# A transformer block on one core: turning probabilities and queries with DVE and DMA instead of TensorE

## The chip, the cores and the metric

The kernel runs on one core of a Trainium2 chip. The metric is the device time of one execution in microseconds (us). TensorE (PE) multiplies, VectorE (DVE), ScalarE (ACT) and GpSimd (POOL) work element by element, SyncE (SP) issues DMAs.

## The reference

One block on a sequence of 256 tokens of width 2048, in float32, followed by a sliding-window attention. Cut to what is computed:

```python
h = x
y = rms(h) ; z = y @ w_in                      # 2048 x 4096
oa, ob, oc, od = four mixers on parts of z     # gated unit, two convolutions, pooling
h = h + concat(oa, ob, oc, od) @ w_out         # 2048 x 2048
y = rms(h) ; h = h + (silu(y @ w_gate) * (y @ w_up)) @ w_down      # 2048 x 5632 and back
y = rms(h) ; h = h + sigmoid(y @ w_ple_gate) * (p @ w_ple_proj)    # 2048 x 2048
h = rms(h)
# attention: 32 heads of 64 in 4 groups, one key/value head per group, window 128
q, k, v, gate = split(rms(h) @ swa_w_in)       # 2048 x 4608
s = rms(q) @ rms(k).T * scale + bias[bucket(distance)]     # blocks of 128 queries x 256 keys
p = exp(s - max(s, sink)) / (sum + exp(sink - max))
out = h + ((p @ v) * silu(gate)) @ swa_w_out   # 2048 x 2048
```

## The kernel before, in words

**Weights.** All weight matrices pass through TensorE in 500 chunks of 256 rows x 512 columns (512 KB). SP loads chunk `s` into `w_raw` (8 slots, `RAW`), ACT rounds it to fp32r in `w_hi` (`split` at L542, 4 slots, `SPL`; the high part), DVE subtracts that from the raw one into `w_lo` (`split` at L867; the low part), and PE makes 12 matmuls of 128x512 from both (`chunk`, L1373 to L1375: low weights, high weights, and high weights with the low part of the activations). ACT waits for PE to be done with chunk `s-4` before it writes the high part of chunk `s`, so ACT and DVE can be up to four chunks ahead of PE. A unit is 8 chunks: 512 output columns.

**Order.** Each engine has its own list, written out by hand: for every chunk `(v, c)` (unit `v`, chunk `c` of it) first the chunk, then what else stands at that place. ACT, DVE and SP wait only by semaphores, in list order. Nothing is reordered.

**Attention.** The attention's input projection is units `v` = 0 to 8, chunks 396 to 467. Unit 0 gives keys and values, units 1 to 4 the queries of head groups `g` = 0 to 3, units 5 to 8 their gates. Head group `g` is worked on from unit `v = g + 3` on, in three rounds (`ROUNDS`): round 0 is the first 128 queries (8 heads, 128 keys), rounds 1 and 2 the last 128 queries (4 heads each, 256 keys). A round is a chain over three engines:

- `score` (PE, L1593) multiplies queries and keys into the banks `sp`;
- `softmax_max` (DVE, L1225 to L1233) adds the bias, finds the largest value and gives the maximum to ACT;
- `exp` (ACT, L772) takes the exponentials in `tile2` or `tile6`, by turns;
- `turn` (PE, `blocks`, L1403) transposes the 128x1024 probabilities in 8 matmuls against the identity, `copy` (ACT, L596) brings them into `tile7`;
- `weigh` (PE, L1614) multiplies them with the values into a bank `tp`, `keep_output` (ACT, L782) copies that out.

The queries are transposed on PE as well (`to_features`, L1393, 8 matmuls) and copied by ACT with their gain (`copy`, gqk). `denominators` (DVE, L1241) sums up. POOL squares the queries (L528), makes their inverse norms (L500, L502) and loads the bias of the next head group.

Elsewhere a 256x512 piece is transposed without PE: `turn` on DVE (L889, 32x32 blocks), then `move` on SP: one DMA to `parked` in DRAM and four back (the blocks put in place).

**Gate of the embedding (`PLE_UNIT`).** Four units before the attention, one after the other. Its first three input pieces are turned by DVE and DMA, the fourth by PE (`H_PLE`, 8 matmuls).

## Time and profile before

| | us |
|---|---|
| median of 3 runs | 1438.45 (1437.99 to 1438.53) |
| the profiled execution's own time | 1438.18 |
| its span, first to last instruction | 1436.4 |
| PE busy | 1428.5 (99%) |
| DVE busy | 881.7 (61%) |
| ACT busy | 702.2 (49%) |
| POOL busy | 52.5 (4%) |

The granted clock of TensorE was 1.00 over the whole span. PE's busy time is modelled from pipelined matmuls: of two matmuls the second starts 0.23 us after the first and each is drawn 0.39 us long, so what a piece of work costs PE is read from start to start, not from the busy column. The attention stage, where most of the change lies, is 1163 to 1313 us of the span; the unit of head group `g` = 2, used below as the example, starts near 1236.

### The profile page before, as it was taken

How to read it: one execution, taken by the hardware profiler on the slowest of the kernel's cores; microseconds unless marked ns; L12 is line 12 of the kernel's file. 1: busy time of each engine (PE TensorE's matmuls, PEld its weight loads, DVE VectorE, ACT ScalarE, POOL GpSimd, SP SyncE). 2: the span in 40 equal slices, each digit the busy share in tenths (PEclk: the TensorE clock that was granted, in tenths of full speed). 3: DMA queues.
4: the chain of work that ended last, by engine and by line, in shares of the span. 5: the costliest groups of instructions: out<-in, count | busy, mean ns of one | idle time of the engine just before them, and what ended most of it. 6: DMA issues, size and time to landing. Idle time of an engine off the chain costs nothing.

```text
span 1436.4 us, 17816 instructions
## 1 busy us (share of the span) xinstructions
PE 1428.5 (99%) x6495; PEld 1171.8 (82%) x6495; DVE 881.7 (61%) x1138; ACT 702.2 (49%) x942; POOL 52.5 (4%) x52
## 2 busy tenths in 40 slices
PE   9999999999999999999999999999999999999999
PEld 7888888888888888888888888888888877777887
DVE  5599976665555554545555545557677666676653
ACT  7444555454444433444443344445556566675442
POOL 2000010000000000000000000000000222110000
PEclk9999999999999999999999999999999999999999
DMA  9766557676766666677665667767677655546762
GB/s 333 224 190 174 179 178 251 216 257 199 231 210 226 223 191 192 193 225 222 220 220 196 193 194 220 222 223 241 230 237 236 208 189 162 169 142 201 264 221 89
DMA packets 160212, 301.28 MB, mean 210 GB/s; under 512 B 10673, under 2 KB 26285, under 8 KB 160024
## 3 DMA queue, kind: packets, MB, share of 16 engines
q1 hardware_dynamic: 158328, 293.76, 64.1%
q0 software_dynamic: 1792, 6.71, 1.5%
q8 instruction: 38, 0.62, 0.2%
q14 instruction: 22, 0.18, 0.0%
q10 hardware_dynamic: 32, 0.01, 0.0%
HBM read 284.65 MB, written 15.78 MB: 209 GB/s over the span
## 4 chain that ended last, share of the span: by engine, by line
PE 96%; DVE 2%; ACT 1%; issue 0%; DMA 0%; ACTq 0%
PE acc L1373 31%; PE acc L1375 30%; PE acc L1374 30%; PE acc L1435 1%; PE tp L1393 1%; PE tp L1614 1%; PE sp L1593 1%; PE tp L1403 1%; ACT tile L772 1%; DVE w_lo L867 1%; DVE tile L1225 0%; ACT w_hi L542 0%; DVE smx L1229 0%; DMA resid<-in_x 0%; PE tp L1425 0%
## 5 line engine op out<-in xcount | busy, mean ns | idle before, releaser
L867 DVE TENSOR_TENSOR w_lo<-w_raw,w_hi 128x1024 fp32r<-128x1024 f32 x500 | 612.4, 1227 | 509.4 <-ACT w_hi L542 508.5
L542 ACT ACTIVATE w_hi<-w_raw 128x1024 fp32r<-128x1024 f32 x500 | 528.7, 1060 | 628.4 <-PE acc L1375 626.5
L1373 PE MATMUL acc<-w_lo,yh 128*128 128x512 f32 x1184 | 461.4, 390 | 0.0
L1375 PE MATMUL acc<-w_hi,yl 128*128 128x512 f32 x1184 | 460.7, 389 | 0.0
L1374 PE MATMUL acc<-w_hi,yh 128*128 128x512 f32 x1184 | 460.6, 389 | 0.0
L1373 PE MATMUL acc<-w_lo,hh 128*128 128x512 f32 x784 | 309.2, 394 | 0.0
L1374 PE MATMUL acc<-w_hi,hh 128*128 128x512 f32 x784 | 305.4, 390 | 0.0
L1375 PE MATMUL acc<-w_hi,hl 128*128 128x512 f32 x784 | 305.4, 390 | 0.0
L1373 PEld LDWEIGHTS acc<-w_lo,yh 128*128 128x128 f32 x1184 | 222.2, 188 | 46.8 <-issue 0.6
L1375 PEld LDWEIGHTS acc<-w_hi,yl 128*128 128x128 f32 x1184 | 222.2, 188 | 46.1
L1374 PEld LDWEIGHTS acc<-w_hi,yh 128*128 128x128 f32 x1184 | 222.3, 188 | 46.0
L1373 PEld LDWEIGHTS acc<-w_lo,hh 128*128 128x128 f32 x784 | 147.1, 188 | 38.9 <-issue 8.6
L1375 PEld LDWEIGHTS acc<-w_hi,hl 128*128 128x128 f32 x784 | 147.2, 188 | 31.1
L1374 PEld LDWEIGHTS acc<-w_hi,hh 128*128 128x128 f32 x784 | 147.2, 188 | 29.3
L945 DVE SCALAR_TENSOR_TENSOR tile<-tile,cw 128x255 f32<-128x255 f32 (+29 forms) x120 | 48.3, 471 | 0.0
L500 POOL TENSOR_SCALAR eps_ms<-ms 128x2 f32<-128x2 f32 (+2 forms) x9 | 5.4, 601 | 958.3 <-DVE ms L929 916.2
L772 ACT ACTIVATE tile<-tile,negm 128x128 f32<-128x128 f32 (+1 forms) x64 | 28.3, 446 | 16.3 <-DVE ssink L1233 16.3
L549 ACT ACTIVATE tile<-acc,rs 128x512 f32<-128x512 f32 x42 | 26.3, 677 | 4.4 <-PE acc L1375 4.4
L923 DVE TENSOR_TENSOR resid<-acc,resid 128x512 f32<-128x512 f32 x38 | 24.4, 683 | 0.0
L502 POOL TENSOR_TENSOR rs<-eps_ms,minus_half 128x2 f32<-128x2 f32 (+2 forms) x12 | 24.0, 1999 | 1.0
L1225 DVE SCALAR_TENSOR_TENSOR tile<-sp,rs,big 128x128 f32<-128x128 f32 (+1 forms) x64 | 21.9, 409 | 2.6 <-PE sp L1593 2.6
L596 ACT ACTIVATE tile<-tp 128x512 f32<-128x512 f32 x30 | 16.1, 587 | 14.4 <-PE tp L1403 8.3
(151 smaller groups left out, 518.9 us busy)
## 6 DMA issues: line engine op xcount, KB each, us to landing
w_raw<-in_w_gate SPq DMA_DIRECT2D x88, 512.0 KB, 4.4
w_raw<-in_w_up SPq DMA_DIRECT2D x88, 512.0 KB, 4.5
w_raw<-in_w_down SPq DMA_DIRECT2D x88, 512.0 KB, 4.3
w_raw<-in_swa_w_in SPq DMA_DIRECT2D x72, 512.0 KB, 4.0
w_raw<-in_w_in SPq DMA_DIRECT2D x64, 512.0 KB, 4.5
w_raw<-in_w_out SPq DMA_DIRECT2D x32, 512.0 KB, 4.5
w_raw<-in_w_ple_gate SPq DMA_DIRECT2D x32, 512.0 KB, 5.2
w_raw<-in_swa_w_out SPq DMA_DIRECT2D x32, 512.0 KB, 5.1
```

Source lines behind the costliest of these rows:

```text
L502: pool.tensor_tensor(rs[:, k, 0:n], eps_ms[:, k, 0:n], minus_half[:, 0:n], ALU.pow).then_inc(got, 1)
L542: act.activation(w_hi[:, s % SPL], w_raw[:, s % RAW], ACT.Copy).then_inc(hi_ready, 1)
L549: last = act.activation(dst[:, t], acc[u % 2][t][:], func, scale=s_)
L596: act.activation(dst[:, 512 * i:512 * (i + 1)], tp[(h + i) % 2][:], ACT.Copy, scale=scale).then_inc(tp_left["a"], 1)
L772: act.activation(sv[:, i], sv[:, i], ACT.Exp, bias=negm[:, n, i:i + 1], accum_out=ssum[:, n, i:i + 1])
L867: dve.tensor_tensor(w_lo[:, s % SPL], w_raw[:, s % RAW], w_hi[:, s % SPL].bitcast(F32), ALU.subtract).then_inc(lo_ready, 1)
L923: last = dve.tensor_tensor(cols, acc[u % 2][t][:], cols, ALU.add)
L945: dve.scalar_tensor_tensor(dst, src, w_, dst, ALU.mult, ALU.add).then_inc(conv, 1)
L1225: last = dve.scalar_tensor_tensor(sv[:, i], src, rs[:, R_Q + g, 8 * t + h:8 * t + h + 1], bias[:, h, 0:w][:, ::-1], ALU.mult, ALU.add)
L1373: pe.matmul(dst, xh[:, f, tk], w_lo[:, s % SPL, k], start=(f == 0), stop=False)
L1374: pe.matmul(dst, xh[:, f, tk], w_hi[:, s % SPL, k], start=False, stop=False)
L1375: last = pe.matmul(dst, xl[:, f, tk], w_hi[:, s % SPL, k], start=False, stop=(f == CK * n - 1))
```

## The change

- **Probabilities.** After `exp`, DVE transposes 32x32 blocks (`turn_probs`, one instruction of 128x1024), SP writes them to DRAM (`put_probs`) and reads them back with the blocks in place (`fetch_probs`, four DMAs). The 8 PE transposes and the two ACT copies of each of the 12 rounds are gone. `weigh` moves back in PE's list: round 0 from `(v,3)` to `(v,7)`, round 1 from `(v,6)` to `(v+1,1)`, round 2 from `(v+1,1)` to `(v+1,3)`.
- **Queries.** The same for the four query tiles (`turn_queries` on DVE, `put_queries` and `fetch_queries` on SP), then ACT scales them into place (`queries_in_place`, at `(v,1)`, where the copy stood at `(v,0)`).
- **Buffers.** Two of the three probability buffers are weight slots: from chunk 396 on, weights turn through 6 slots of `w_raw`, not 8.
- **POOL.** In each of the units 3 to 6 the low parts of chunks 4 and 6 are made by POOL (`weights_low`).
- **Gate units woven.** The four units of the embedding's gate are taken in the order `DOWN` (6 chunks of unit 0, 6 of unit 1, then the rest of both), and the fourth input piece is turned by DVE and DMA too: 8 PE transposes less.
- SP's moves are cut into a put and a later fetch.

```diff
+ATT = START[SWA_UNIT]
+ATT_SLOTS = [(ATT + i) % RAW for i in range(RAW - 2)]
+SPARE_SLOTS = [(ATT - 2) % RAW, (ATT - 1) % RAW]
+POOL_LOW = [ATT + 8 * v + c for v in range(3, 7) for c in (4, 6)]
...
+                    if c == 1 and 3 <= j <= 6:
+                        put_queries(j - 3)
...
+                    if c == 3 and 3 <= j <= 6:
+                        fetch_queries(j - 3)
+                    if c == 3 and 4 <= j <= 7:
+                        put_probs(3 * (j - 4))
...
+                    if c == 5 and 4 <= j <= 7:
+                        fetch_probs(3 * (j - 4))
+                        put_probs(3 * (j - 4) + 1)
...
+            def weights_low(i):
+
+                for s in POOL_LOW[2 * i:2 * i + 2]:
+                    pool.wait_ge(hi_ready, s + 1)
+                    pool.tensor_tensor(w_lo[:, s % SPL], w_raw[:, slot(s)], w_hi[:, s % SPL].bitcast(F32),
+                                       ALU.subtract).then_inc(low_by_pool, 1)
...
+            def queries_in_place(g):
+
+                act.wait_ge(q_in, 64 * (g + 1))
+                if g:
+                    act.wait_ge(scores, 3 * g)
+                src = queries.rearrange("p (q k t n) -> p k t q n", q=4, k=4, t=T)
+                for t in range(T):
+                    last = act.activation(quarters(feat(4))[:, :, t], src[:, :, t], ACT.Copy, scale=gqk[:, 0:1])
+                last.then_inc(q_ready, 1)
...
-                    if c == 0 and 3 <= v <= 6:
-                        copy(H_Q[v - 3], tile[4], gqk[:, 0:1])
...
-                        copy(H_PT[v - 4, 2], tile[7])
+                    if c == 0 and 5 <= v <= 8:
+                        keep_output(v - 5, 2)
+                    if c == 1 and 3 <= v <= 6:
+                        queries_in_place(v - 3)
...
+            def turn_probs(g, r):
+
+                n = 3 * g + r
+                dve.wait_ge(expd, n + 1)
+                if n >= 3:
+                    wait_half(dve, H_PV[g - 1, r])
+                dve.transpose(probs[n % 3].rearrange("p (r b n) -> p b r n", r=4, n=32),
+                              tile[(2, 6)[n % 2]][:].rearrange("p (b r n) -> p b r n", r=4, n=32)).then_inc(p_blocks, 1)
...
                     if c == 1 and 4 <= v <= 7:
+                        turn_probs(v - 4, 2)
                         denominators(v - 4, 2)
                     if c == 1 and 3 <= v <= 6:
                         softmax_max(v - 3, 0)
+                    if c == 3 and 2 <= v <= 5:
+                        turn_queries(v - 2)
                     if c == 3 and 3 <= v <= 6:
                         softmax_max(v - 3, 1)
...
                     if c == 5 and 3 <= v <= 6:
+                        turn_probs(v - 3, 0)
                         softmax_max(v - 3, 2)
...
                     if c == 7 and 3 <= v <= 6:
+                        turn_probs(v - 3, 1)
                         denominators(v - 3, 1)
...
                 if r == 0:
-                    wait_half_left(pe, H_Q[g] + 1)
+                    pe.wait_ge(q_ready, g + 1)
...
                     if c == 1 and 4 <= v <= 7:
+                        weigh(v - 4, 1)
+                    if c == 2 and 3 <= v <= 6:
+                        score(v - 3, 2)
+                    if c == 3 and 4 <= v <= 7:
                         weigh(v - 4, 2)
```

DVE's list from the low part of chunk `(v,7)` to the next group's first bias addition, before (L867 is a low part, `rden` the denominators, `ms` the query norms, `sp` the scores):

```order
L867 TENSOR_TENSOR w_lo<-w_raw,w_hi 128x1024
L1208 TENSOR_REDUCE ms<-tile 128x16
L1241 TENSOR_TENSOR rden<-ssum,ssink 128x4
L1242 RECIPROCAL rden<-rden 128x4
L867 TENSOR_TENSOR w_lo<-w_raw,w_hi 128x1024 x2
L1241 TENSOR_TENSOR rden<-ssum,ssink 128x4
L1242 RECIPROCAL rden<-rden 128x4
L1225 SCALAR_TENSOR_TENSOR tile<-sp,rs,big 128x128 x8
```

The same stretch of DVE's list now (L967 is the low part, L1330 `turn_probs`):

```order
L967 TENSOR_TENSOR w_lo<-w_raw,w_hi 128x1024
L1330 STREAM_TRANSPOSE w_raw<-tile 128x8x4x32
L1365 TENSOR_TENSOR rden<-ssum,ssink 128x4
L1366 RECIPROCAL rden<-rden 128x4
L967 TENSOR_TENSOR w_lo<-w_raw,w_hi 128x1024 x2
L1330 STREAM_TRANSPOSE w_raw<-tile 128x8x4x32
L1365 TENSOR_TENSOR rden<-ssum,ssink 128x4
L1366 RECIPROCAL rden<-rden 128x4
L1349 SCALAR_TENSOR_TENSOR tile<-sp,rs,big 128x128 x8
```

Two transposes stand in the stretch that had none; the query norms have moved one chunk forward.

ACT's list from the exponentials of round 2 to those of the next group's round 0, before (L542 is a high part, L596 with `gqk` the queries, other L596 the probabilities, L782 `keep_output`):

```order
L774 ACTIVATE ssink<-ssink 128x4
L782 ACTIVATE wide<-tp 128x4x128
L542 ACTIVATE w_hi<-w_raw 128x1024
L596 ACTIVATE tile<-tp 128x512 x2
L542 ACTIVATE w_hi<-w_raw 128x1024
L596 ACTIVATE tile<-tp,gqk 128x512 x2
L542 ACTIVATE w_hi<-w_raw 128x1024
L782 ACTIVATE wide<-tp 128x2x128
L542 ACTIVATE w_hi<-w_raw 128x1024
L596 ACTIVATE tile<-tp 128x512 x2
L772 ACTIVATE tile,ssum<-tile,negm 128x128 x8
```

The same stretch of ACT's list now (L635 is the high part, L886 `queries_in_place`):

```order
L868 ACTIVATE ssink<-ssink 128x4
L635 ACTIVATE w_hi<-w_raw 128x1024 x2
L877 ACTIVATE wide<-tp 128x2x128
L635 ACTIVATE w_hi<-w_raw 128x1024
L886 ACTIVATE tile<-wide,gqk 128x4x128 x2
L635 ACTIVATE w_hi<-w_raw 128x1024
L866 ACTIVATE tile,ssum<-tile,negm 128x128 x8
```

The copies of the probabilities are gone; the queries are made ready after three high parts instead of two.

## Rows read from the trace of the kernel before

**Rows 1.** Stretch 1197:1230: busy us and count of each engine, clock, DMA share, GB/s.

```profile
1197.00:1230.00 33.00, 33.00 (x182) 24.69 (x181) 21.79 (x44) 21.77 (x56) 7.22 (x5) 1.00 0.54 159
```

**Rows 2.** Waits of PE in the attention stage: us in total, times, longest.

```profile
PE tp L1403 <- ACT wide L782: 2.3, 2, 1.5
```

**Rows 3.** Timeline of PE: start us, us, what, xcount.

```profile
1226.44 0.40 PE L1375 MATMUL acc<-w_hi,hl 128*128 128x512 f32 x1
1226.67 1.04 PE L1393 MATMUL tp<-ident,tile 128*128 128x128 f32 x8
...
1227.78 0.39 PE L1374 MATMUL acc<-w_hi,hh 128*128 128x512 f32 x1
...
1230.41 1.16 PE L1593 MATMUL sp<-tile 64*128 64x128 f32 x16
...
1263.24 0.49 PE L1593 MATMUL sp<-tile 64*128 64x128 f32 x4
```

**Rows 4.** Timeline of ACT, head group 2, from the exponentials of round 0.

```profile
1236.99 0.40 ACT L772 ACTIVATE tile<-tile,negm 128x128 f32<-128x128 f32 x1
...
1240.17 1.05 ACT L542 ACTIVATE w_hi<-w_raw 128x1024 fp32r<-128x1024 f32 x1
1241.12 1.25 ACT L549 ACTIVATE tile<-acc,rr 128x512 f32<-128x512 f32 x2
...
1245.80 0.51 ACT L772 ACTIVATE tile<-tile,negm 128x256 f32<-128x256 f32 x1 [0.24 <-DVE ssink L1233]
...
1247.88 1.04 ACT L542 ACTIVATE w_hi<-w_raw 128x1024 fp32r<-128x1024 f32 x1
...
1253.50 0.51 ACT L772 ACTIVATE tile<-tile,negm 128x256 f32<-128x256 f32 x1 [2.67 <-DVE ssink L1233]
...
1255.59 0.57 ACT L782 ACTIVATE wide<-tp 128x512 f32<-128x512 f32 x1
```

**Rows 5.** Timeline of DVE, head group 2.

```profile
1231.67 2.16 DVE L1225 SCALAR_TENSOR_TENSOR tile<-sp,rs,big 128x128 f32<-128x128 f32 x8 [0.60 <-PE sp L1593]
...
1241.25 1.22 DVE L867 TENSOR_TENSOR w_lo<-w_raw,w_hi 128x1024 fp32r<-128x1024 f32 x1 [4.55 <-ACT w_hi L542]
1242.39 1.65 DVE L1225 SCALAR_TENSOR_TENSOR tile<-sp,rs,big 128x256 f32<-128x256 f32 x4
...
1250.10 1.65 DVE L1225 SCALAR_TENSOR_TENSOR tile<-sp,rs,big 128x256 f32<-128x256 f32 x4
...
1259.49 0.15 DVE L1241 TENSOR_TENSOR rden<-ssum,ssink 128x4 f32<-128x4 f32 x1
...
1259.88 1.22 DVE L867 TENSOR_TENSOR w_lo<-w_raw,w_hi 128x1024 fp32r<-128x1024 f32 x1
```

**Rows 6.** Timeline of DVE, block transposes and a low part beside POOL.

```profile
1147.56 1.30 DVE L889 STREAM_TRANSPOSE wide<-tile 128x512 f32<-128x512 f32 x2
1148.78 1.18 DVE L867 TENSOR_TENSOR w_lo<-w_raw,w_hi 128x1024 fp32r<-128x1024 f32 x1
1150.30 2.50 DVE L867 TENSOR_TENSOR w_lo<-w_raw,w_hi 128x1024 fp32r<-128x1024 f32 x1 [0.34 <-ACT w_hi L542]
```

**Rows 7.** Timeline of POOL: the squares of head groups 0 and 2.

```profile
1148.79 2.93 POOL L528 TENSOR_TENSOR tile<-tile 128x1024 f32<-128x1024 f32 x1 [3.87 <-ACT tile L549]
...
1242.44 1.90 POOL L528 TENSOR_TENSOR tile<-tile 128x1024 f32<-128x1024 f32 x1 [11.37 <-ACT tile L549]
```

**Rows 8.** DMA issues, whole span: count, KB each, median us to landing.

```profile
parked<-tile SPq DMA_DIRECT2D x25, 512.0 KB, 5.1
tile<-parked SPq DMA_DIRECT2D x100, 128.0 KB, 2.7
```

**Rows 9.** Head group 0's first exponential (ACT).

```profile
1171.38 0.40 ACT L772 ACTIVATE tile<-tile,negm 128x128 f32<-128x128 f32 x1 [2.61 <-DVE ssink L1233]
```

**Rows 10.** Table loads of ACT beside `exp`, 1163:1310: count, busy us, mean ns.

```profile
L772 ACT ACT_TABLE_LOAD x2 | 2.6, 1283 | 0.0
```

**Rows 11.** Timeline of PE: first matmul of chunk (7,4).

```profile
1313.16 0.39 PE L1373 MATMUL acc<-w_lo,hh 128*128 128x512 f32 x1
```

More of the change, by code:

```diff
@@ L170, in build @@
     parked = nc.dram_tensor("parked", (P, 1024), F32, kind="Internal").ap()
+    parked_q = nc.dram_tensor("parked_q", (P, 1024), F32, kind="Internal").ap()
+    parked_p = [nc.dram_tensor(f"parked_p{i}", (P, 1024), F32, kind="Internal").ap() for i in range(3)]
     with ExitStack() as ctx:
@@ L277, in build @@
         turned = sem("turned")
+        low_by_pool = sem("low_by_pool")
+        p_blocks = sem("p_blocks")
+        p_out = [sem(f"p_out{i}") for i in range(3)]
+        p_in = [sem(f"p_in{i}") for i in range(3)]
+        q_blocks = sem("q_blocks")
+        q_out = sem("q_out")
+        q_in = sem("q_in")
+        q_ready = sem("q_ready")
         blocks_out = sem("blocks_out")
@@ L292, in wait_unit, with wait_low @@
             eng.wait_ge(used, LAST_CHUNK[u] + 8 * lap.oct)
+        def wait_low(eng, s, lap=ONCE):
+            if s in POOL_LOW:
+                eng.wait_ge(low_by_pool, POOL_LOW.index(s) + 1)
+            else:
+                eng.wait_ge(lo_ready, s + 1 - sum(1 for i in POOL_LOW if i < s) + 8 * lap.oct)
         def taker(h):
```

317 lines of the change are left out of this document (169 added, 148 removed).

## The prediction

> **What bounds the kernel now.** I read the page first: PE is 99% busy, all else far from full, and the granted clock is 1.00. Next the stretches of the attention stage: in one period of 33 us DVE and ACT are each 21.8 us busy and the DMA share is 0.54, so nothing but PE is near its limit [rows 1]. Third, PE's waits: in the whole stage 2.3 us, two waits of PE's transposes for ACT's `keep_output` [rows 2]. So PE's own work is the end of the kernel: what leaves PE's list is a gain, as long as the others deliver in time. Last I followed one period through ACT and DVE, since the change gives DVE work and takes away PE's: that decides here. The period of a head group is 1263.24 - 1230.41 = 32.83 us [rows 3].
>
> **What leaves PE.** From the last matmul before a group of 8 transposes (1226.44) to the second one behind it (1227.78) are 1.34 us; without the group these would be two steps of 0.23 [rows 3]. A group costs 1.34 - 0.46 = 0.88 us. The change removes 12 groups of probabilities, 4 of queries, 1 of the embedding's gate: 17 x 0.88 = 15.0 us, and the two waits, 2.3. Where round 0's `score` stood right before a `weigh` (1230.41 and the group at its end), both now stand alone, an estimated 0.2 us each for switching in and out, three times: -0.6. If nothing else came late, the profiled execution would go from 1438.18 to 1438.2 - 15.0 - 2.3 + 0.6 = 1421.5 us. PE's work in a period would be 32.83 - 4 x 0.88 + 0.2 = 29.5 us.
>
> **What then comes late: the ring of `softmax_max` and `exp`.** ACT and DVE hold the softmax and the parts of the weights in one list each, so the three rounds of a group and the first of the next are one ring, which can't turn faster than its own sum. I count from the first exponential of round 0 (1236.99 in the example).
>
> Leg 1, to the first exponential of round 1. Exponentials 1236.99 to 1240.17: 3.18. High part, then DVE's low part, beside it ACT's `take` (1241.12 + 1.25): until 1242.39, 2.22. New: `turn_queries`, two 128x512 block transposes, which start the next instruction 1148.78 - 1147.56 = 1.22 later [rows 6]. They stand before round 1's bias additions and wait for the `take`, which ends at the same moment. Then softmax, 1242.39 to the exponential at 1245.80: 3.41. Sum 10.03, before 8.81 [rows 4, 5].
>
> Leg 2, to round 2. Exponentials 2.08 (1245.80 to 1247.88), high and low part 2.22 (1247.88 to 1250.10), new `turn_probs` of round 0: one 128x1024 transpose, taken as the pair, 1.2. Softmax 1250.10 to 1253.50: 3.40. Sum 8.90, before 7.70 [rows 4, 5].
>
> Leg 3, to the next group's round 0. Exponentials 2.09 (1253.50 to 1255.59); high and low part of chunk 7, 2.22; `turn_probs` 1.2; denominators 0.39 (1259.49 to 1259.88); low parts of chunks 0 and 1, 2 x 1.14 (as 1241.25 to 1242.39) = 2.28; `turn_probs` of round 2, 1.2; denominators 0.39; softmax of round 0, 3.41 + 2.16 - 1.65 = 3.92. Sum 13.69. Before, it took 32.83 - 8.81 - 7.70 = 16.32: there DVE waited for ACT, whose list held three pairs of copies and waits for PE's transposes. So the removed copies pay here, and DVE becomes the one behind which ACT stands [rows 3 to 5].
>
> The ring: 10.03 + 8.90 + 13.69 = 32.6 us. The old period is 32.83. The gain of 3.3 us per period on PE is nearly all given back: PE waits 32.6 - 29.5 = 3.1 us in each, and I can say where. `queries_in_place` comes after three high parts (0.95 each, 1240.17 to 1241.12) and takes about 1.25 as the `take` does, so round 0's `score` of the next group is released at 10.03 + 8.90 + 2.09 + 2.85 + 1.25 = 25.1 us of the ring. The first group has no `weigh` beside it. Its own first `score` stands 1.26 (1230.41 to 1231.67) + 3.92 = 5.2 us before its first exponential, at 1170.5 (below), and PE needs from there 3 scores of about 1.25 and 8 chunks of 2.72, 25.5 us: it is back at 1190.8, and the release is at 1170.5 + 25.1 = 1195.6: a gap of 4.8 us [rows 3, 5].
>
> **What is left of the gain.** The low parts were ready well before PE wanted them; that lead is used up, once. In the clock of the old trace: group 0's first exponential comes 0.88 earlier (its query transposes go), at 1171.38 - 0.88 = 1170.5 [rows 9]. Three turns of 32.62 bring group 3's to 1268.4. Its leg 1 has no query transposes but two table loads of 1.28 [rows 10] (the gate's `take` is a silu) and lasts about 9.7; leg 2 8.9; exponentials, high and low part 2.09 + 2.22: the low part of chunk (6,7) is ready at 1291.3. PE waits for it, needs 2.72 for the chunk (12 x 0.227, the step of rows 3) and then wants round 0's turned probabilities at 1294.0. Their fetch stands behind the load that waits for that same low part: issued at 1291.3, 2.7 to land [rows 8], and the fourth is issued after the first, I take 4: 1295.3. Then three `weigh` of about 1.2 and four chunks: chunk (7,4) starts at 1295.3 + 3.6 + 10.9 = 1309.8, where it was 1313.16 [rows 11]. That is 3.4 us, with 0.88 of the embedding's gate 4.2. Behind it the list is PE's alone, as before. 1438.18 - 4.2 = 1434.0 us; the old median is 0.3 above the profiled execution, which I leave aside.
>
> **The other parts.** POOL's eight low parts, 8 x 1.22 us off DVE, are not on the ring's sum (the stretch around chunks 4 and 6 has none on DVE now), but without them it would be 2.3 us longer per turn. POOL took 1.90 us for 128x1024 with one tensor read twice and 2.93 beside a low part of DVE [rows 7]; PE wants chunk 4 over 5 us after its high part, so POOL itself hides at either price. The block transposes to and fro: a put lands in 5.1, a fetch in 2.7 [rows 8]; queries are put near 8 us of the ring, fetched near 14 and needed near 24, cover 5 us and more. The six slots instead of eight: a load is issued when the low part six chunks earlier is done and has over 10 us until its high part; a put of as many bytes lands in 5.1 [rows 8]. DMA traffic rises from 0.54 of the time by four moves of 1 MB on 5.2 MB per period, to about 0.54 x 9.4 / 5.2 = 0.97 if the small packets cost as the mean does, and less if as weights: that is near full, and the one place where cover could vanish. `weigh` now reads its moving operand in runs of 32 instead of 128 elements; no row shows that. From nothing to a doubling of 1 us per `weigh`; I take nothing, since PE has 3 us to spare per period, and keep +2 us for the last three. The woven gate units: 0.88 gained, the turned piece has five chunks of 2.72 for 5.1 + 2.7.
>
> **A rule against it.** While POOL squared the queries of group 0, DVE's low part took 2.50 instead of 1.22, and POOL 2.93 instead of 1.90; group 2's square lay beside a bias addition (one operand in PSUM) and both kept their time [rows 5 to 7]. By this rule, the trace agrees. The Trainium skill, "GPSIMD Engine Reference", Specifications, says that GpSimd shares its SBUF interfaces with VectorE and that it contends with DVE instructions in a two-port mode or with two SBUF inputs. By my walk POOL's low parts run at 7 to 9 and 14 to 16 us of the ring, where DVE has bias additions, reductions and a transpose, so the sum keeps 1.22.
>
> **Rivals.**
>
> PE stays the bound: the ring turns faster than I count (transposes cheap, ACT ahead), and most of 16.7 us arrives: 1421.5 to 1431. For it: all views show PE as the bound. Against: every item but the transposes is a start-to-start of the trace, and to reach 29.5 the three block transposes and the queries' 1.22 would have to cost 0.4 us each. Chance 0.15.
>
> Not much changes: the DMA load near 0.97 delays a fetch by 2 us per group, or the gaps of 3 to 5 us on PE, longer than any wait of before (1.5, rows 2), let its clock fall from 2.4 to 1.2 GHz. A chunk at the lower level takes 2.72 us more. In the first three groups that hides (PE is 3 us early again), behind the last gap it doesn't: 1434.0 + 2.7 = 1436.7. The Trainium skill, "TensorE: Matmul & The Clock Gate", section "Why this matters for your kernels", warns of such gaps between bursts; no row here shows a fall. Within 0.2% (about what a measurement of this kernel tells from no change): 1435.6 to 1441.3. Chance 0.15.
>
> Slower, by the shared port: POOL's low parts and square slide onto DVE's low parts of chunks 3, 5 and 7. Each meeting adds 2.50 - 1.22 = 1.28 to the ring. Two per turn in 3.3 turns are 8.4: 1442.4; three 1446.6. It decides from 2.2 us per turn on. For it: DVE is to be 21.8 + 4 x 1.2 - 2 x 1.22 = 24 us busy of 32.6. Against: the places above. Chance 0.15.
>
> **Numbers.** The ring as counted 0.55, with 1431 to 1437.5 (each of the four transposes off by 0.2 moves 2.6 us), of it 0.13 within 0.2%. Faster 0.42 + 0.15 = 0.57, same 0.13 + 0.15 = 0.28, slower 0.15. The range that leaves out the far ends: 1426 to 1441.
>
> **What would show it.** Right: PE waits of 3 to 5 us before round 0's `score` for ACT's `queries_in_place`, in units 3 to 5; the same group's first exponentials 32.6 apart; DVE without pause from the low part of chunk 7 to round 0's softmax; margin of the low parts before PE near zero at chunk (6,7). Wrong: scores less than 31 us or more than 34 apart; PE waits named for DMAs; low parts of 2.5 us on DVE; a clock below 1.00.

## The result: slower by 0.45%, and the profile after

The changed kernel takes 1444.86 us (median of 6 runs, 1442.79 to 1446.56), the kernel before 1438.19 in the runs beside it (1437.99 to 1438.53). The ratio is 1.0045, with a 95% interval of 1.0034 to 1.0056: 6.7 us slower. The forecast was 1434.0 us (1426 to 1441) and faster. The profiled execution took 1445.09 us, its span 1443.4, which is 7.0 more than before.

The stretches of the attention stage after, the columns as in [rows 1] (busy us and count of PE, PEld, DVE, ACT, POOL; granted clock, DMA share, GB/s):

```profile
1163.00:1197.00 34.00, 28.84 (x135) 22.40 (x133) 21.88 (x41) 20.53 (x51) 10.43 (x6) 0.95 0.63 193
1197.00:1230.00 33.00, 30.62 (x141) 22.21 (x142) 24.22 (x47) 18.64 (x52) 11.09 (x7) 0.90 0.92 290
1230.00:1263.00 33.00, 30.25 (x146) 21.45 (x145) 24.23 (x48) 18.73 (x51) 10.87 (x7) 0.95 0.90 279
1263.00:1296.00 33.00, 31.26 (x158) 22.50 (x157) 25.42 (x46) 21.51 (x53) 4.88 (x2) 1.00 0.82 258
1296.00:1320.00 24.00, 18.22 (x85) 12.83 (x83) 16.73 (x21) 11.59 (x14) 0.00 (x0) 1.00 1.03 302
```

The second row answers to [rows 1]: PE executes 141 matmuls where it executed 182 (recorded ones), DVE is busy 24.22 us as forecast (24), and the DMA share is 0.92 instead of 0.54. PE's waits in the stage, the answer to [rows 2]:

```profile
PE sp L1714 <- ACT tile L886: 8.1, 3, 4.1
PE tp L1730 <- DMA tile<-parked_p: 7.0, 3, 3.0
PE tp L1730 <- DMA w_raw<-parked_p: 2.8, 2, 1.9
```

2.3 us have become 17.9. The first line (`score` for `queries_in_place`) was forecast; the 9.8 us of the other two, `weigh` waiting for its probabilities to land, were not, and are one of the signs that the prediction had named for being wrong. The last row of the table above has a granted clock of 1.00: from 1263 us on nothing of the loss is the clock's.

Where the time is lost can be read off five starts of ACT: round 0 of the four head groups and round 2 of the last (start, us, instruction).

```profile
1173.92 0.40 ACT L866 ACTIVATE tile<-tile,negm 128x128 f32<-128x128 f32 x1 [3.83 <-DVE ssink L1357]
...
1206.62 0.40 ACT L866 ACTIVATE tile<-tile,negm 128x128 f32<-128x128 f32 x1 [6.44 <-DVE ssink L1357]
...
1239.34 0.40 ACT L866 ACTIVATE tile<-tile,negm 128x128 f32<-128x128 f32 x1 [6.18 <-DVE ssink L1357]
...
1272.06 0.40 ACT L866 ACTIVATE tile<-tile,negm 128x128 f32<-128x128 f32 x1 [5.11 <-DVE ssink L1357]
...
1291.68 0.51 ACT L866 ACTIVATE tile<-tile,negm 128x256 f32<-128x256 f32 x1 [4.72 <-DVE ssink L1357]
```

They cut the stage into four pieces that can be compared in every kernel: the start of the first exponential, three turns of the ring, two more legs in group 3, and the tail from there to chunk (7,4), after which PE's list is full in these two (123.2 us to the end of the span before, 123.3 after). The prediction counts 1170.5 and 1309.8 in the clock of the old trace and takes the 0.88 us of the gate units off at its end; in the table they are taken off at once, so that its column can be set beside a trace.

| us | before | forecast | after |
|---|---|---|---|
| first exponential | 1171.38 | 1169.6 | 1173.92 |
| three turns | 98.4 | 97.9 | 98.1 |
| group 3, legs 1 and 2 | 17.6 | 18.6 | 19.6 |
| tail to chunk (7,4) | 25.8 | 22.8 | 28.5 |
| chunk (7,4) | 1313.16 | 1308.9 | 1320.14 |

So the turns were right to 0.1 us each, and 11.2 us were missed, nearly all at both ends: 4.3 at the start, 1.0 in the last legs, 5.7 in the tail, 0.2 in the turns. The forecast 1434.0 and the profiled 1445.09 us are 11.1 apart.

### The profile page after: what moved, and what is told of

Same layout as the page of the kernel before. It is cut to its first block, busy times and chain, and to the rows that moved or that the text cites. A ratio compares the mean times of both kernels' runs of the same rounds, so it can differ in the third digit from the quotient of the medians.

```text
span 1443.4 us, 17640 instructions
## 1 busy us (share of the span) xinstructions
PE 1420.0 (98%) x6359; PEld 1161.9 (80%) x6359; DVE 893.6 (62%) x1156; ACT 690.1 (48%) x918; POOL 67.8 (5%) x60
## 4 chain that ended last, share of the span: by engine, by line
PE 86%; DVE 6%; ACT 3%; DMA 2%; issue 1%; SPq 0%; POOL 0%; DVEq 0%; ACTq 0%
PE acc L1501 28%; PE acc L1503 28%; PE acc L1502 28%; ACT tile L866 2%; DVE tile L1349 2%; PE acc L1563 1%; DVE w_lo L967 1%; DVE smx L1353 1%; ACT w_hi L635 1%; DMA parked_p<-w_raw 1%; DMA wide<-parked_q 1%; DVE w_raw L1330 0%; PE tp L1521 0%; DMA parked_q<-wide 0%; SPq L426 0%
## 5 line engine op out<-in xcount | busy, mean ns | idle before, releaser
L967 DVE TENSOR_TENSOR w_lo<-w_raw,w_hi 128x1024 fp32r<-128x1024 f32 x492 | 601.3, 1226 | 509.3 <-ACT w_hi L635 508.6
L635 ACT ACTIVATE w_hi<-w_raw 128x1024 fp32r<-128x1024 f32 x500 | 527.5, 1059 | 635.5 <-PE acc L1503 633.0
L697 ACT ACTIVATE tile<-resid 128x512 f32<-128x512 f32 x32 | 19.8, 622 | 7.7 <-DVE resid L1284 5.1
L1714 PE MATMUL sp<-tile 64*128 64x128 f32 (+1 forms) x128 | 15.5, 379 | 8.1 <-ACT tile L886 8.1
```

The lines of the kernel that those rows point to most:

```text
L635: act.activation(w_hi[:, s % SPL], w_raw[:, slot(s)], ACT.Copy).then_inc(hi_ready, 1)
L697: act.activation(tok(junk)[:, t], resid[:, t, CW * j:CW * (j + 1)], ACT.Square, accum_out=ssq[:, row, t, j:j + 1]).then_inc(squares, 1)
L967: dve.tensor_tensor(w_lo[:, s % SPL], w_raw[:, slot(s)], w_hi[:, s % SPL].bitcast(F32), ALU.subtract).then_inc(lo_ready, 1)
L1714: last = pe.matmul(sp[i % 2][:, w * (i // 2):w * (i // 2) + w], feat(4)[rows_, h // 2, P * t:P * (t + 1)], feat(3)[rows_, g, 0:w], start=T ...
```

## The experiments

Each has its expectation as it was on record, and the time of the kernel before beside it is 1438.2 to 1438.5 us.

**The start.** After, ACT's `keys()` is the row to read. First row: ACT's copy of the turned keys; the second is `queries_in_place`. The bracket is the idle time before the instruction:

```profile
1161.56 1.15 ACT L682 ACTIVATE tile<-wide 128x512 f32<-128x512 f32 x2 [6.74 <-DMA wide<-parked]
...
1166.50 1.33 ACT L886 ACTIVATE tile<-wide,gqk 128x512 f32<-128x512 f32 x2 [0.94 <-DMA wide<-parked_q]
```

Before, this copy started at 1157.00, after 1.29 us of waiting. The keys' fetch had moved two loads down SP's list.

```diff
 # e1_keys
-                    if (j, c) == (3, 0):
-                        put(T_K)
-                    if (j, c) == (3, 2):
-                        fetch(T_K)
+                    if (j, c) == (3, 0):
+                        move(T_K)
```

> The changed kernel, but SP fetches the turned keys right behind their put, at chunk (3,0), and not two loads later; nothing else moves. Theory 1, the ring: the first head group's exponentials started at 1173.9 and not at 1170.5 because ACT's list stood 6.7 us in keys() behind that late fetch; every later group follows at 32.7 us, so the whole end comes 3.4 us earlier: 1444.9 to about 1441.5. Theory 2, the landings: the end is set by the turned probabilities that arrive late for the last three weigh, whatever the first group does; then under 1 us. Theory 3, the clock: PE's gap of 3.8 us before the first score goes, and with it the slow matmuls behind it (0.8 us); then another 0.8 on top of 3.4.

Measured: 1443.02 us (1441.58 to 1443.6), ratio 1.0032 [1.0020, 1.0045]; the first exponential at 1171.83, turns of 32.71. The first exponential comes 2.1 us earlier and the median falls by 1.8; the intervals of the two kernels overlap, but in the traces chunk (7,4) starts 2.3 us earlier too. About 2 us of the 6.7 come from here, where the first theory had 3.4. In this execution the clock also fell in the tail, behind a wait of 3.5 us.

**The clock.** After the long waits PE's matmuls follow each other in twice the time. Two groups of PE, before and after the wait for group 1's queries:

```profile
1194.66 0.39 PE L1502 MATMUL acc<-w_hi,hh 128*128 128x512 f32 x1
1194.88 0.39 PE L1503 MATMUL acc<-w_hi,hl 128*128 128x512 f32 x1
1199.38 2.08 PE L1714 MATMUL sp<-tile 64*128 64x128 f32 x16 [4.11 <-ACT tile L886]
...
1201.98 0.63 PE L1502 MATMUL acc<-w_hi,hh 128*128 128x512 f32 x1
1202.41 0.63 PE L1503 MATMUL acc<-w_hi,hl 128*128 128x512 f32 x1
```

A step is 0.22 us before the wait and 0.43 after it: the level of 1.2 GHz instead of 2.4, and the granted clock of this stretch is 0.90. The experiment fills the waits with products that nobody reads.

```diff
 # e2_warm: in score, and spin(tp[h % 2], 6) in front of round 0's weigh
                 if r == 0:
+                    spin(sp[0], (12, 14, 10, 8)[g])
                     pe.wait_ge(q_ready, g + 1)
```

> The changed kernel, but PE fills its gaps with matmuls of 128x512 whose result is not used (12, 14, 10 and 8 before the four first scores, 6 before each round 0 weigh), 0.23 us each. Theory 3, the clock: the matmuls at 1.2 GHz (0.43 instead of 0.23 us, about 6 us in all in the changed kernel) are lost time, the clock stays at 2.4 GHz and the time falls by up to 6 us, to 1439. Theory 1, the ring: PE has 3 us to spare in each turn, the slow stretches lie in that spare time, and the time stays within 1.5 us of 1444.9; the granted clock goes to 1.00 all the same, and the exponentials keep their 32.7 us.

Measured: 1445.02 us (1442.72 to 1448.65), ratio 1.0046 [1.0033, 1.0060]. The clock was held in four of the five stretches (the columns as above; 0.86 stands in the last):

```profile
1197.00:1230.00 33.00, 30.38 (x153) 21.69 (x152) 24.23 (x47) 18.62 (x51) 11.07 (x7) 1.00 0.91 287
1230.00:1263.00 33.00, 33.00 (x165) 24.01 (x164) 24.23 (x48) 18.91 (x52) 11.05 (x7) 1.00 0.96 295
...
1296.00:1320.00 24.00, 19.46 (x77) 13.92 (x76) 15.07 (x19) 10.04 (x12) 0.00 (x0) 0.86 1.00 291
```

The turns stayed at 32.71 us and the median did not move. In the turns the slow clock lay in time that PE had to spare. In the tail of the profiled execution (1447.86 us, above the median) the clock fell behind a wait of 3.2 us: from its second `weigh` to its third PE took 9.3 us without a wait, where the changed kernel took 7.7 with one of 0.9. So a fall that comes behind the last turn costs time, some 1.7 us here. The changed kernel's own profiled tail had no fall.

**POOL's low parts.**

```diff
 # e3_no_pool
-POOL_LOW = [ATT + 8 * v + c for v in range(3, 7) for c in (4, 6)]
+POOL_LOW = []
```

> The changed kernel without POOL's eight low parts: DVE makes them all. Theory 1, the ring: two low parts per turn come back to DVE's list, both behind a wait of ACT's, 1.14 us each: 32.7 becomes 34 to 35 us, the time rises by 4 to 8 us to 1449 to 1453. Rival, the shared port: POOL's 2.4 us low parts slow DVE or deliver late to PE, and without them the time falls or stays.

Measured: 1443.82 us (1442.0 to 1445.28), ratio 1.0038 [1.0024, 1.0052], not told apart from the changed kernel. The expected 1449 to 1453 did not come. The turns are 32.71 with POOL or without: the two low parts per turn were never on the ring, and the prediction's "2.3 us longer" without them is wrong. One leg did change, group 3's first, 10.57 to 9.57 us. DVE after, and POOL beside it, around that leg's softmax:

```profile
1279.17 1.22 DVE L1353 TENSOR_REDUCE smx<-tile 128x4 f32<-128x1024 f32 x1
1280.42 1.91 DVE L1355 TENSOR_TENSOR smx<-smx,sinks 128x4 f32<-128x4 f32 x1
```

```profile
1279.91 2.40 POOL L608 TENSOR_TENSOR w_lo<-w_raw,w_hi 128x1024 fp32r<-128x1024 f32 x1 [17.09 <-ACT w_hi L635]
```

And DVE without POOL's part:

```profile
1278.02 1.22 DVE L1353 TENSOR_REDUCE smx<-tile 128x4 f32<-128x1024 f32 x1
1279.27 0.16 DVE L1355 TENSOR_TENSOR smx<-smx,sinks 128x4 f32<-128x4 f32 x1
```

An operation on 4 elements per partition takes 1.91 us instead of 0.16 and ends at 1282.33, when POOL ends (1279.91 + 2.40 = 1282.31). DVE's two-tensor operation waited out POOL's. That is the mechanism of the third rival, once in this kernel, for 1.0 us of the leg.

**The ring shortened.** Three of DVE's transposes go to places where it waits for ACT: behind the softmax of the same chunk, and a chunk earlier for round 1.

```diff
 # e4_ring
-                        turn_probs(v - 4, 2)
-                        denominators(v - 4, 2)
                     if c == 1 and 3 <= v <= 6:
                         softmax_max(v - 3, 0)
+                    if c == 1 and 4 <= v <= 7:
+                        turn_probs(v - 4, 2)
+                        denominators(v - 4, 2)
...
-                    if c == 3 and 2 <= v <= 5:
-                        turn_queries(v - 2)
                     if c == 3 and 3 <= v <= 6:
                         softmax_max(v - 3, 1)
+                    if c == 3 and 2 <= v <= 5:
+                        turn_queries(v - 2)
...
                     if c == 6 and 3 <= v <= 6:
+                        turn_probs(v - 3, 1)
                         denominators(v - 3, 0)
-                    if c == 7 and 3 <= v <= 6:
-                        turn_probs(v - 3, 1)
                         denominators(v - 3, 1)
```

> The changed kernel, but three of DVE's four transposes per turn stand where DVE waits for ACT anyway: the queries' behind round 1's softmax instead of before it, round 1's probabilities at chunk 6 instead of 7, round 2's behind the next group's first softmax instead of before it. Theory 1, the ring: the turn loses 1.22 + 1.24 + 1.24 = 3.7 us and becomes 29.0, less than PE's own 29.5; the time falls by 3.2 in each of three turns, 9 to 10 us, to about 1435. Theory 2, the landings: at a DMA share of 0.92 in 1197:1230 a shorter turn finds no room, PE's waits for the turned probabilities grow, and the time falls by 3 us at most.

Measured: 1446.94 us (1443.55 to 1450.14), ratio 1.0056 [1.0042, 1.0070]. The turns below are those of its profiled execution, the slowest of the five (1450.14 us). The first turn is 31.05 us where 29.0 was expected, the next two are 34.53 and 37.73. What the first one lacks stands in three rows, POOL's and then DVE's:

```profile
1179.65 2.38 POOL L608 TENSOR_TENSOR w_lo<-w_raw,w_hi 128x1024 fp32r<-128x1024 f32 x1
```

```profile
1180.69 1.37 DVE L1355 TENSOR_TENSOR smx<-smx,sinks 128x4 f32<-128x4 f32 x1
...
1199.46 2.16 DVE L1349 SCALAR_TENSOR_TENSOR tile<-sp,rs,big 128x128 f32<-128x128 f32 x8 [1.33 <-DMA big<-bias_rows]
```

Without the queries' transposes before it, round 1's softmax comes 1.2 us earlier and meets POOL's low part: the small operation takes 1.37 us instead of 0.17 and ends with POOL's (1182.06, 1182.03). So leg 1 stays at 10.02 us. The second row is a wait of 1.33 us for the bias rows in leg 3. No run has the shortened ring without POOL's low parts. Three waits of this kernel in the stage, DVE's and SP's (us in total, times, longest):

```profile
DVE tile L1349 <- DMA big<-bias_rows: 11.7, 3, 5.6
```

```profile
SPq L426 <- DMA parked_p<-w_raw: 25.8, 6, 6.8
SPq L436 <- DVE wide L1321: 17.5, 3, 6.8
```

The bias rows (1 MB, issued when the group before has used its own) take the ring's place (waits of 1.3, 4.7 and 5.6 us), and SP now stands in front of the queries' put with the weight loads behind it (17.5 us, 2.5 in the changed kernel). Two more kernels take these apart: SP's list refitted (puts of queries one load and of round 2 one load later, round 0's fetch one earlier, keys as in e1_keys), and the same without the bias rows of groups 1 to 3 (it leaves their loads out and uses group 0's for all).

```diff
 # f3_ring2, SP, on e1_keys and e4_ring together
-                    if c == 1 and 3 <= j <= 6:
+                    if c == 2 and 3 <= j <= 6:
                         put_queries(j - 3)
...
+                    if c == 4 and 4 <= j <= 7:
+                        fetch_probs(3 * (j - 4))
                     if c == 5 and 4 <= j <= 7:
-                        fetch_probs(3 * (j - 4))
                         put_probs(3 * (j - 4) + 1)
...
                         fetch_probs(3 * (j - 4) + 1)
-                        put_probs(3 * (j - 4) + 2)
+                    if c == 0 and 5 <= j <= 8:
+                        put_probs(3 * (j - 5) + 2)
```

```diff
 # f4_ring2_nobias, against f3_ring2
-                    load_bias(g)
...
-                    dve.wait_ge(bias_in, 16 * (g + 2))
+                    dve.wait_ge(bias_in, 16 * 2)
```

> The changed kernel with the keys' fetch right behind its put, with DVE's turning of queries and one turning of probabilities outside the ring, and with the puts and fetches in SP's list refitted to that (first theirs moved later, round 0's fetch one load earlier), so that SP does not stand before a put. Ring theory: ring 31.0 to 31.5 us instead of 32.7, three turns give 4 to 5 us on the 1443.0 of the kernel with the keys' fetch alone: 1438 to 1439. Landing theory: the bias rows' transfer (10 to 12 us to land beside a DMA share of 0.9) ends the ring instead, rings 33 to 35 us: 1443 to 1447.

> As the one before, but the bias rows of groups 1 to 3 are not fetched (group 0's stand for all: part of the computation is changed), 3 transfers of bias rows less. Landing theory: with the bias out of the ring the rings fall to 31 us and the time to 1436 to 1439, at least 4 us below the kernel with these loads. Ring theory: no difference between the two (within 1 us), since the ring was DVE and ACT work in both.

Measured: 1444.18 us (1442.91 to 1445.91), ratio 1.0040 [1.0027, 1.0054], with turns of 31.53, 32.00 and 36.76; and 1438.81 us (1436.82 to 1440.88), ratio 1.0002 [0.9993, 1.0011], with turns of 31.51, 31.33 and 30.88. Three transfers of 1 MB cost 5.4 us once the ring is short enough to meet them. In `f3_ring2` DVE waits no longer for the rows themselves; ACT waits for the queries' fetch, 5.5 us in two waits, 4.5 of them in the third turn, and without the rows there is no such wait. In both kernels round 1's small operation meets POOL's low part in all four groups (0.84 to 1.91 us instead of 0.17), as in `e4_ring`. In the changed kernel itself the ring is too long for that:

```diff
 # g3_no_bias, against the changed kernel
-                    load_bias(g)
...
-                    dve.wait_ge(bias_in, 16 * (g + 2))
+                    dve.wait_ge(bias_in, 16 * 2)
```

> The changed kernel with nothing but the bias rows of groups 1 to 3 not fetched (group 0's stand for all: part of the computation is changed). Landing theory: DMA share in the stage falls from 0.90 to about 0.82, the fetches of probabilities land 1 us earlier and PE's waits before weighing shrink from 9.8 us to about 5: 1440 to 1442 us with rings still 32.7. Ring theory: the bias rows were in time in the changed kernel (rings 32.7 without a wait for them), so no more than 1 us: 1444 to 1445.

Measured: 1443.19 us (1442.03 to 1445.91), ratio 1.0034 [1.0021, 1.0048]; turns 32.72. The waits before `weigh` fell from 9.8 to 4.4 us, as the landing theory had it, but those for scores rose from 8.1 to 12.5. In the profiled execution (1445.81 us) the tail is 27.4 us instead of 28.5, and the first exponential comes 1.7 later, behind a longer wait for the keys (7.70). The intervals overlap: this run is inconclusive on the time.

**One part of the change at a time, on the kernel before.** `f1_woven` has the woven gate units alone. `f2_queries` has the queries by DVE and DMA, with PE still turning probabilities. `g1_both` has both. The queries' part isn't quite the change's: here their transposes stand behind round 1's softmax and not before it, their put and fetch two loads later, and `queries_in_place` one chunk earlier.

```diff
 # f1_woven, PE (SP, ACT and DVE follow the same order DOWN)
-            for j in range(NG):
-                for c in range(8):
-                    u = PLE_UNIT + j
...
-                        to_features(H_PLE, resid[:, :, 3 * CW:])
+            for n, (j, c) in enumerate(DOWN):
+                if j == 0 and c in (0, 2, 4, 6):
+                    pe.wait_ge(turned_lo, T_PLE + c // 2 + 1)
+                chunk(START[PLE_UNIT] + n, PLE_UNIT + j, c, yh, yl)
```

```diff
 # f2_queries, PE
-                    if c == 5 and 2 <= v <= 5:
-                        wait_left(pe, u - 1)
-                        to_features(H_Q[v - 2], tok(1))
 # DVE
                     if c == 3 and 3 <= v <= 6:
                         softmax_max(v - 3, 1)
+                    if c == 3 and 2 <= v <= 5:
+                        turn_queries(v - 2)
 # SP
+                    if c == 3 and 3 <= j <= 6:
+                        put_queries(j - 3)
+                    if c == 5 and 3 <= j <= 6:
+                        fetch_queries(j - 3)
```

> The kernel before with one part of the change alone: the gate units' chunks woven, so that PE does not turn four tiles there. Ring theory: PE reaches the round-0 softmax one group of four transposes (0.88 us) earlier, the ring of the maximum, exponential, sums and turning is as long as before (32.7 to 32.8 us a turn), nothing new is late: 1438.2 - 0.9 = 1437.3 us. Landing theory (DMA transfers that land late cost the time): this part adds no transfer, so the same 1437.3. If the four values tiles that are now fetched later meet other transfers, the keys wait as in the whole change (some 3 us): 1441. Of the whole change's +6.7 us this part then explains half.

> The kernel before with one other part alone: queries are turned by DVE inside blocks and by two DMA passes between them; PE still turns the probabilities (12 groups) and four groups of queries go away. PE-bound theory: 4 x 0.88 = 3.5 us less of PE's work, and PE waited only 2.3 us in this stage before: 1438.2 - 3.5 = 1434.7 us, as long as the ring stays at 32.7 us or less. Ring theory: the ring has about the length of PE's turn before (32.8 against 32.7), and the turning of queries adds 1.24 us of DVE a turn to it where it stands (third chunk), so the ring gets 33.0 to 34.0 and the gain is used up: 1437 to 1439. Landing theory: the DMA share rises from 0.54 to about 0.65 only, no weigh waits.

> The kernel before with woven gate units and with queries turned by DVE and DMA in all four groups; PE turns the probabilities as before. If the parts add: 1438.3 - 0.8 (woven alone) - 0.65 (queries alone) = 1436.9 us, first exponential near 1172.3, rings 31.9. Against the changed kernel (1444.9) the difference is what turning the probabilities by DVE and DMA costs: 8 us. If instead the parts of the change cost time only together, this one is near 1440.

Measured: woven 1437.55 us (1437.19 to 1438.8), ratio 0.9996 [0.9986, 1.0005]; queries 1437.68 (1436.89 to 1438.92), 0.9995 [0.9986, 1.0004]; both 1436.81 (1435.88 to 1438.97), 0.9990 [0.9981, 0.9999]. Woven starts the first exponential at 1170.60, 0.78 earlier, with no longer wait for the keys (0.8 us, 1.3 before): this part is as forecast and innocent, though its time alone isn't told apart from the kernel before. Nor is that of the queries alone. With the queries, each turn is 31.90 instead of 32.8 us: PE is full there and one group of transposes per turn (0.9) is gained in full, where the ring theory had 33 to 34 us. Leg 1 keeps its 8.82 us: behind the softmax the queries' transposes cost the ring nothing. But the first exponential comes at 1173.13, 1.75 later than before where it should come 0.88 earlier, and eats most of it. The cause is again a fetch; ACT, `queries_in_place` for group 0 in the kernel with queries alone:

```profile
1165.76 1.33 ACT L811 ACTIVATE tile<-wide,gqk 128x512 f32<-128x512 f32 x2 [4.58 <-DMA wide<-parked_q]
```

So its put goes ahead of the keys' fetch:

```diff
 # g2_both_early, SP, against g1_both
                 sp_.dma_start(parked[:, :], src).then_inc(blocks_out, 16)
+                if between is not None:
+                    between()
                 sp_.wait_ge(blocks_out, 16 * (n + 1) + 16 * lap.turns)
...
-                        move(T_K)
+                        move(T_K, between=lambda: put_queries(0))
...
+                    if (j, c) == (3, 4):
+                        fetch_queries(0)
```

> As the one before, but the put of the first group's queries goes ahead of the fetch of the keys' tile, and their fetch one load earlier. In the kernel with queries alone, ACT waited 4.6 us for this fetch with two splits of chunks behind it, and the first exponential came 2.5 us later than before. Landing theory: the first exponential falls to 1169.8 to 1170.5 us, rings stay at 31.9, and the time is 2 to 2.5 us below the kernel without this edit: 1434.6 us, which beats both kernels. PE-bound theory: PE sets the end of the stage anyway and the late first score only used up PE's spare time, within 0.5 us of the kernel without the edit.

Measured: 1434.44 us (1433.85 to 1435.88), ratio 0.9974 [0.9964, 0.9985]: **faster than both kernels**. SP's list there, the keys' put, the queries' put and the two fetches with a weight load between them; then ACT:

```profile
1148.02 0.34 SPq L391 DMA_DIRECT2D parked<-wide  x1
1150.34 0.34 SPq L402 DMA_DIRECT2D parked_q<-wide  x1
1151.75 1.77 SPq L397 DMA_DIRECT2D wide<-parked  x4
1153.57 0.94 SPq L381 DMA_DIRECT2D w_raw<-in_swa_w_in  x2
1154.56 1.90 SPq L409 DMA_DIRECT2D wide<-parked_q  x4
```

```profile
1162.00 1.34 ACT L818 ACTIVATE tile<-wide,gqk 128x512 f32<-128x512 f32 x2 [1.72 <-DMA wide<-parked_q]
...
1169.63 0.40 ACT L798 ACTIVATE tile<-tile,negm 128x128 f32<-128x128 f32 x1 [2.61 <-DVE ssink L1282]
```

(The "2.5 us later than before" of this expectation was 1.75; 2.5 is the distance to the kernel with woven units.) The first exponential is at 1169.63, 3.1 us earlier than in `g1_both` and where the forecast had it (1169.6), the turn 31.89. This kernel is the changed one with the turning of probabilities, POOL's low parts and the two lent slots taken out again, the queries' transposes, put and fetch placed as above, and the first fetches in order.

**The tail.** The last turn of the changed kernel, SP and then PE:

```profile
1288.20 0.34 SPq L446 DMA_DIRECT2D parked_p<-tile  x1
...
1296.59 1.89 SPq L426 DMA_DIRECT2D tile<-parked_p  x4
1298.53 0.43 SPq L446 DMA_DIRECT2D parked_p<-w_raw  x1
...
1304.02 1.75 SPq L426 DMA_DIRECT2D w_raw<-parked_p  x4
1305.82 0.43 SPq L446 DMA_DIRECT2D parked_p<-w_raw  x1
...
1312.59 1.75 SPq L426 DMA_DIRECT2D w_raw<-parked_p  x4
```

```profile
1302.78 1.08 PE L1730 MATMUL tp<-tile 128*64 128x512 f32 x4 [3.01 <-DMA tile<-parked_p]
1303.79 0.50 PE L1501 MATMUL acc<-w_lo,hh 128*128 128x512 f32 x1
...
1311.46 1.08 PE L1730 MATMUL tp<-w_raw,tile 128*64 128x256 f32 x8 [1.89 <-DMA w_raw<-parked_p]
...
1319.13 1.08 PE L1730 MATMUL tp<-w_raw,tile 128*64 128x256 f32 x8 [0.88 <-DMA w_raw<-parked_p]
```

A fetch lets PE begin 6.2 to 7.4 us after its issue (1296.59 to 1302.78, 1304.02 to 1311.46, 1312.59 to 1319.13), not 4. And the three stand in one list, each fetch behind its put's landing and each next put behind the fetch: fetches 7.4 and 8.6 us apart. PE's three `weigh` start 8.7 and 7.7 us apart, without the waits 6.8. Can an earlier fetch, or a later use, mend it?

```diff
 # g4_keys_fetch, SP, on e1_keys
+                    if c == 4 and 4 <= j <= 7:
+                        fetch_probs(3 * (j - 4))
                     if c == 5 and 4 <= j <= 7:
-                        fetch_probs(3 * (j - 4))
                         put_probs(3 * (j - 4) + 1)
```

```diff
 # h1_later, PE, on e1_keys: rounds 0, 1, 2 after chunks 0, 2, 4 (ahead of this 7, 1, 3)
+                    if c == 0 and 4 <= v <= 7:
+                        weigh(v - 4, 0)
+                    if c == 2 and 4 <= v <= 7:
+                        weigh(v - 4, 1)
+                    if c == 4 and 4 <= v <= 7:
+                        weigh(v - 4, 2)
...
```

> The changed kernel with the keys' fetch right behind its put (1443.0 alone) and round 0's probabilities fetched one load earlier in SP's list. If SP's place in its list makes the fetch late, PE's waits before weighing (8.6 us, longest 3.5) fall to 5 or less and the last turn ends 2 to 3 us earlier: 1440 to 1441 us. If the landing itself (5 to 6 us beside a DMA share of 0.9) makes it late, the earlier place only waits for the put's landing and holds SP's weight loads back: 1442.5 to 1444.

> The changed kernel with the keys' fetch right behind its put (1443.0 alone) and each weighing one chunk later on PE (rounds 0, 1, 2 after chunks 0, 2, 4 of the next unit; ahead of this, after 7, 1, 3). If the fetches of probabilities land after PE has come to them and that costs the last turn its time, PE works a chunk (2.72 us) instead of waiting: the waits before weighing (8.6 us) fall to 3 or less, the stretch from group 3's last exponential to chunk (7,5) shrinks by 2 to 3 us, and the time is 1440 to 1441.5. If these waits only take up time that PE would spend waiting for scores or for the next landing, the waits move to the scores and the time stays within 1 us of 1443.0.

Measured: the earlier fetch 1445.02 us (1444.17 to 1446.34), ratio 1.0046 [1.0032, 1.0060], 2.0 slower than `e1_keys`: SP stands before the put's landing, with the loads behind it, and two turns stretch to 33.4 and 33.1. The later use 1440.40 us (1439.15 to 1441.79), ratio 1.0016 [1.0006, 1.0025], 2.6 faster than `e1_keys`. PE's waits there:

```profile
PE sp L1712 <- ACT tile L884: 11.2, 4, 4.8
PE tp L1728 <- DMA w_raw<-parked_p: 2.0, 1, 2.0
PE tp L1728 <- DMA tile<-parked_p: 0.9, 1, 0.9
```

8.6 us before `weigh` have become 2.9. In the turns the waits went to the scores (6.9 to 11.2) and gained nothing; from group 3's last exponential (1289.57, now 1289.20) to chunk (7,5) (1320.73, now 1316.94) it is 27.7 instead of 31.2 us (31.3 in the changed kernel, whose tail had no fall of the clock). Last, the order of the first put on top:

```diff
 # h2_later_early, SP, on h1_later
                     if (j, c) == (3, 0):
-                        move(T_K)
+                        put(T_K)
+                        put_queries(0)
+                        fetch(T_K)
+                    if (j, c) == (3, 2):
+                        fetch_queries(0)
```

> As the one before, and the first group's queries are put ahead of the keys' fetch and fetched one load earlier, which took 2.4 us from the kernel with queries and woven units. Landing theory: first exponential at about 1169.7 instead of 1171.8 us, rings 32.7, so 2 us less than the kernel without it: 1438 to 1439.5, no faster than the kernel before, because the ring is 32.7 us with the probabilities' turning in it (31.9 without) and group 3's two legs take 19.6 us instead of 17.6. If the late start were hidden, no more than 0.5 us less.

Measured: 1438.54 us (1437.17 to 1439.32), ratio 0.9998 [0.9989, 1.0007], the first exponential at 1169.42, turns of 32.72. With the first transfers and the late probabilities both mended, the whole change is worth nothing.

## Why the prediction was wrong

**PE's work leaves: right.** The turned groups are gone, and `weigh` with its operand in runs of 32 costs the same (before, then after, PE in the stage):

```profile
L1614 PE MATMUL tp<-tile 128*64 128x256 f32 (+1 forms) x80 | 13.0, 437 | 0.0
```

```profile
L1730 PE MATMUL tp<-w_raw,tile 128*64 128x256 f32 x64 | 8.7, 392 | 2.8 <-DMA w_raw<-parked_p 2.8
L1730 PE MATMUL tp<-tile 128*64 128x512 f32 x16 | 4.3, 618 | 7.0 <-DMA tile<-parked_p 7.0
```

13.0 us in both, and from a `weigh` to the chunk behind it 1.01 us in both (after: 1311.46 to 1312.47). The +2 us kept for it were not needed.

**The ring: right.** Legs 10.03, 9.05 and 13.63, forecast 10.03, 8.90 and 13.69; a turn 32.72 for 32.62. The transposes take 1.24 us. That they are what lengthens the ring is borne out by `e4_ring`, where leg 3 without two of them fell to 11.97 in spite of a wait of 1.33. The first gap of PE before a `score` was 4.50 us for 4.8. The claim on POOL within it was wrong (`e3_no_pool`).

**"Group 0's first exponential comes 0.88 earlier": failed, 4.3 us** with the 0.88 of the gate units, which belong before it too. I took the removed transposes off the start and left the transfers in their place out of it. The keys' fetch stood two loads later and ACT waited 6.7 us for it; mending it gave 2 us (`e1_keys`), and putting the queries ahead of it another 1.9 (`h2_later_early` against `h1_later`; 2.4 in `g2_both_early` against `g1_both`). With both mended the first exponential stands at 1169.42, the forecast being 1169.6: the transposes' gain was there, the two fetches hid it.

**"Leg 1 lasts about 9.7": 0.9 too short** by one DVE instruction that waited for POOL; without POOL it was 9.57. The place was one of those that I had called free of meetings, since I looked only for low parts against low parts. The price was off too: a meeting costs what is left of POOL's operation, 0.7 to 1.7 us for the small operation in these runs, and not a fixed 1.28. That the third rival's range, 1442.4 to 1446.6, holds the measured time is luck: it wanted 2.2 us in every turn, and the turns of the changed kernel have none.

**"2.7 to land, and the fourth is issued after the first, I take 4", and chunk (7,4) from that: the term that failed most, 5.7 us in the tail.** The 2.7 are the median of [rows 8], over the whole span, where the DMA share is mostly 0.6 to 0.7; in the changed kernel's tail it is 1.03. Fetches let PE begin 6.2 to 7.4 us after their issue, and I counted one landing, not three round trips in a row. The 5.7 us divide into 0.6 for a first fetch issued later behind group 3's last exponential (4.9 us for 4.3), 2.2 for its landing (6.2 for 4) and 2.8 for the two waits that I had not counted (1.9 and 0.9). `h1_later` shows that the probabilities' landing costs time in the tail and not in the turns: its turns are the same, and its gain of 2.6 us lies in the tail. In the traces the tail is 3.4 us shorter than in `e1_keys`, where a fall of the clock is part of it, and 3.6 shorter than the changed kernel's, where none is.

**The DMA share** was worked out as 0.97 and measured at 0.92, 0.90 and 0.82 in the turns. The working stood under a rival of 0.15, with 2 us for it; it belonged in the main sum. The fall of the clock was seen as that rival has it, hidden in the turns. In the profiled tail of the changed kernel it did not come; where it did, in `e2_warm`, it cost about 1.7 us, for the rival's 2.7. How often it falls there in the other executions stays open.

**"The low parts' lead is used up" as the gain: too kind.** The changed kernel's lead was used up as forecast, at chunk (6,7), whose low part was ready 0.75 us before PE wanted it (4.9 before the change). But PE got little for it, since it then stood before its probabilities: chunk (7,4)'s low part was ready 10.9 us early after, and 0.6 before. The bound had moved from PE and the weights to the way of the probabilities.

The sum closes: 4.3 + 0.2 + 1.0 + 5.7 = 11.2 us between 1308.9 and 1320.14. The two single parts of the change are worth 1.7 us together (`g1_both`), 4.0 with the first put in order; the rest of the change, the probabilities' way with POOL's low parts and the keys' later fetch, costs 8.1 (1444.9 against 1436.8): it takes those 1.7 back and 6 more. The keys' order (2 us), the tail and the last legs are named above.

## What to carry to other kernels

Work that is moved from a full engine to DMA returns as a latency, and it is paid where nothing runs ahead: at the first group and behind the last one. Cut such a stage into start, turns, last legs and tail, and take each landing time at the load that the change itself makes, with all round trips that stand in one queue's list. Then move the first puts and fetches ahead of unrelated ones, no further than the put's landing allows (`g4_keys_fetch` lost 2.0 us by it), and uses a step later before anything is given up: here that took 6.3 us off, and the part that still did not pay, the probabilities, was left out of the fastest kernel.

## What the runs showed of the hardware

- Transfers landed later where more ran beside them. The bias rows (1 MB) land in a median of 6.5 us before and 9.6 after; the probabilities' fetches (128 KB each, four to a tile) take a median of 3.8 and 5.0 by the buffer, where [rows 8] have 2.7 for the same form.
- DVE's two-tensor operation on 128x4 elements took 1.91 us when it began 0.5 us into POOL's 128x1024 subtraction, and ended with it; in `e4_ring` two more, begun 1.0 and 1.5 us into it, took 1.37 and 0.91 and ended with it. [rows 6] and [rows 7] read the same way: POOL's square ended at 1151.72, and DVE's low part, begun at 1150.30, 1.08 later. Tensor reductions, bias additions with an operand in PSUM and transposes beside POOL kept their times (1.22, 0.48, 1.24). The Trainium skill, "GPSIMD Engine Reference", Specifications, names contention for two SBUF inputs; the trace agrees, and shows that the wait is what is left of POOL's operation, whatever the size of DVE's.
- POOL took 2.38 to 2.50 us for a 128x1024 low part from two tensors, where the square of one took 1.90.
- In the changed kernel PE's matmul step was 0.43 instead of 0.22 us, for 3 to 6 us, behind waits of 3.4, 4.1 and 2.2 us in the turns; behind the wait of 3.0 us in the tail it stayed at 0.23. Filling the waits held the clock at 1.00 in the turns, and the median stayed the same. In the tail of `e2_warm` a fall behind a wait of 3.2 us cost about 1.7.
